# Experts' down rows laid seven to a partition, with every seventh gate and up column as a stationary block

## The reference, cut to what matters

```python
def swiglu(x, w_gate, w_up, w_down):
    return (jax.nn.silu(x @ w_gate) * (x @ w_up)) @ w_down

# moe_swiglu: D_EXPERT = 3584, all float32
for e in range(N_EXPERTS):
    y = y + combine[:, e:e + 1] * swiglu(xt, w_gate[e], w_up[e], w_down[e])
```

## Time and profile before

| | |
|---|---|
| median of 3 runs | 2860.66 us (2859.99 to 2863.47) |
| the profiled execution's own time | 2862.23 us |
| its span, first to last instruction | 2860.5 us |
| mean granted clock of TensorE, as a share of 2.4 GHz | 0.964 |
| PE busy, PEld busy, DVE busy, ACT busy | 93%, 77%, 24%, 15% |
| moved by DMA | 571.23 MB, mean 200 GB/s |

### The profile page before, as it was taken

How to read it: one execution, slowest core, us unless ns; L and a number is a source line. 1 busy time by engine, 2 the same in 40 slices (tenths; PEclk the granted TensorE clock), 3 DMA queues, 4 the chain that set the end, 5 groups by cost and what they waited for, 6 DMA issues and landing times. The chain is left out here.

```text
span 2860.5 us, 76137 instructions
## 1 busy us (share of the span) xinstructions
PE 2653.4 (93%) x34649; PEld 2200.0 (77%) x34649; DVE 673.8 (24%) x1724; ACT 430.1 (15%) x1039; POOL 88.0 (3%) x168
## 2 busy tenths in 40 slices
PE   8899999989989999999999999899989789878998
PEld 7677777768779999989989978666667577766664
DVE  5411000271120110110110111400043576752001
ACT  1111000110110110100110111400012344431000
POOL 0100000010000000000000000000000000010000
PEclk9899999989989999999999999999999798889999
DMA  7334443534339999999999993374541000002442
GB/s 223 113 130 133 132 153 126 166 118 135 145 116 404 407 408 407 407 407 407 407 408 407 407 366 103 98 221 155 173 131 56 5 7 7 4 4 96 148 160 88
DMA packets 290526, 571.23 MB, mean 200 GB/s; under 512 B 18326, under 2 KB 181141, under 8 KB 290405
## 3 DMA queue, kind: packets, MB, share of 16 engines
q1 hardware_dynamic: 290404, 569.49, 55.0%
HBM read 568.37 MB, written 5.28 MB: 201 GB/s over the span
## 5 line engine op out<-in xcount | busy, mean ns | idle before, releaser
L1738 PE MATMUL ps<-xg,ring 128*64 128x80 f32 x14336 | 517.3, 234 | 8.3 <-issue 3.0
L1738 PEld LDWEIGHTS ps<-xg,ring 128*64 128x64 f32 x14336 | 504.3, 137 | 19.4 <-DMA ring<-in_moe_w_up_dram 9.3
L1333 PE MATMUL ps<-xT,ring 128*128 128x256 f32 x1728 | 379.8, 379 | 4.7 <-PEq L452 3.1
L1333 PEld LDWEIGHTS ps<-xT,ring 128*128 128x128 f32 x1728 | 328.0, 190 | 65.9 <-issue 22.4
L1345 PE MATMUL ps<-ring,hidden 128*128 128x512 f32 x688 | 301.8, 592 | 0.0
L1754 PE MATMUL ps<-hidden,expert_down 128*64 128x80 f32 x7168 | 260.0, 233 | 9.7 <-DVE hidden L1830 5.7
L1754 PEld LDWEIGHTS ps<-hidden,expert_down 128*64 128x64 f32 x7168 | 251.9, 137 | 15.7 <-DVE hidden L1830 7.6
L1345 PEld LDWEIGHTS ps<-ring,hidden 128*128 128x128 f32 x688 | 130.7, 190 | 147.5 <-issue 145.4
L618 PE MATMUL ps<-ring,xT 128*128 128x256 f32 (+1 forms) x1056 | 228.2, 379 | 7.5 <-PEq L1214 3.9
L618 PEld LDWEIGHTS ps<-ring,xT 128*128 128x128 f32 x1056 | 198.3, 195 | 36.1 <-issue 9.3
L618 PE MATMUL ps<-xT,ring 128*128 128x256 f32 (+1 forms) x944 | 214.4, 389 | 10.2 <-PEq L596 4.5
(11 more groups left out here) (380 smaller groups left out, 2482.6 us busy)
## 6 DMA issues: line engine op xcount, KB each, us to landing
ring<-in_moe_w_gate_dram SPq DMA_DIRECT2D x128, 896.0 KB, 16.4
ring<-in_moe_w_up_dram SPq DMA_DIRECT2D x128, 896.0 KB, 16.7
expert_down<-in_moe_w_down_dram SPq DMA_DIRECT2D x96, 1024.0 KB, 17.0
ring<-in_mlp_w_dram SPq DMA_DIRECT2D x64, 1024.0 KB, 5.4
ring<-in_w_xkv_dram SPq DMA_DIRECT2D x16, 1024.0 KB, 5.3
expert_down<-in_moe_w_down_dram SPq DMA_DIRECT2D x32, 512.0 KB, 16.5
ring<-in_ffn_w_gate_dram SPq DMA_DIRECT2D x11, 1024.0 KB, 5.3
ring<-in_ffn_w_up_dram SPq DMA_DIRECT2D x11, 1024.0 KB, 5.3
```

The lines of the kernel that those rows point to most:

```text
L1333: mm = pe.matmul(bank[:, m * SEQ:(m + 1) * SEQ], w[:, c, m * P:(m + 1) * P], self.xT[:, c, :], start=(c == 0), stop=(c == KC - 1))
L1738: mm = pe.matmul(bank[b][o:o + HEAD, at, :], w[:, c, f * P + o:f * P + o + HEAD], xg[:, p * E_STEP + c, :], start=(p == 0 and c == 0 and a ...
```

## The change

On the DRAM side, down rows are taken as (chunk k, partition p, block f): row 896k + 7p + f goes to partition p. A partition's rows of a piece are then neighbours in DRAM. To keep the sum right, hidden column 7m + f must stand on partition m of block f, so the stationary operand of block f in gate and up is made of columns f, 7 + f, 14 + f, ..., that is every seventh column of the piece as it lies on chip, 28 bytes apart. The gate and up transfers stay as they are, and so do the number and the sizes of the matmuls, and their order.

```diff
-        self.expert_src = [I[name][0].rearrange("e (c p) f -> e p c f", p=P) for name in ("moe_w_gate", "moe_w_up", "moe_w_down")]
+        self.expert_src = [I[name][0].rearrange("e (c p) f -> e p c f", p=P) for name in ("moe_w_gate", "moe_w_up")]
+
+        self.expert_src.append(I["moe_w_down"][0].rearrange("e (k p f) d -> e p k f d", p=P, f=E_WIDE // P))
...
-    def load_expert_out(self, sp, p, e, rows):
-        src = self.expert_src[2][e, :, rows, :].rearrange("a p c f -> p (a c) f")
+    def load_expert_out(self, sp, p, e, k):
+        first = sum(E_DOWN[:p])
+        src = self.expert_src[2][e, :, k, first:first + E_DOWN[p], :].rearrange("a p b f d -> p (a b f) d")
         sp.dma_start(self.expert_out(p), src).then_inc(self.expert_loaded[2][p].sem, 16)
...
-                        self.load_expert_out(sp, p, e, slice(first, first + E_DOWN[p]) if k is None else bass.ds(k * FB + first, E_DOWN[p]))
+                        self.load_expert_out(sp, p, e, slice(0, 1) if k is None else bass.ds(k, 1))
...
-                                w = self.expert_in(kind, p)
+                                w = self.expert_in(kind, p).rearrange("p c (m f) -> p c f m", f=FB)
...
-                                            mm = pe.matmul(bank[b][o:o + HEAD, at, :], w[:, c, f * P + o:f * P + o + HEAD], xg[:, p * E_STEP + c, :],
+                                            mm = pe.matmul(bank[b][o:o + HEAD, at, :], w[:, c, f, o:o + HEAD], xg[:, p * E_STEP + c, :],
```

More of the change, by code:

```diff
@@ L1478, in expert_ahead_gate @@
         for p in range(len(E_DOWN)):
-            first = sum(E_DOWN[:p])
-            self.load_expert_out(sp, p, slice(0, 1), slice(first, first + E_DOWN[p]))
+            self.load_expert_out(sp, p, slice(0, 1), slice(0, 1))
     def expert_ahead_up(self, sp):
```

## The result

The changed kernel takes 3173.53 us (median of 4 runs, 3172.32 to 3174.76) against 2862.06 us beside it on the same chip (4 runs). The ratio is 1.1089, with a 95% interval from 1.1072 to 1.1107: 11% slower, 311 us more.

A forecast was written before the change was run, and what follows sets the result against it. Weight transfers were taken to bound the expert stage, with TensorE close behind. Stepped loads at 56.0 ns make TensorE the pace, adding 227.6 and 38.4 us, together 266, with the transfers' gain worth nothing: 3127 us, range 2850 to 3390.

The forecast's parts named there:

- The transfers pace the stage, TensorE has 1.5 us of room in a chunk: Expert stage: weight transfers set 27.04 us a chunk; TensorE has only 5.9 us of room an item, 1.5 a chunk.
- the sum: Whole kernel: seven items grow 227.6 us, the first 38.4, together 266 us, giving 3127 us.
- the plateau of 404 to 408 GB/s: Expert stage before the change: the DMA rate was read as 404 to 408 GB/s from slice 13 to 24.
- the item at TensorE's pace: Expert stage before the change: the first item, loaded ahead, was said to run at TensorE's pace, 103.0 us.
- The longer runs are worth 6 us (0 to 8): Down transfers: 24 packets fewer per engine a chunk at 8 ns save 6 us, only while transfers pace the stage.
- A stepped load costs one more column time for each column: Gate and up stationary loads: 0.83 ns more a column, 112 ns a pair, 56.0 ns a load; chance 0.50.
- Two halves keep side by side: Gate and up loads: two halves of 64 columns still overlap when stepped; without overlap a load would take 112 ns.
- The plateau falls to 313 GB/s, transfers land within 7 us, the clock stays: Expert stage, profile after: rate from 407 to 313 GB/s, transfers landing some 7 us or less after issue, clock 1.00.
- The free case: Gate and up loads: stepping is free or hidden and the longer runs pay, 2854 us; chance 0.23.
- The heavier case: Gate and up loads: stepped halves hinder each other, 90 ns more a load, up to 3393 us; chance 0.13.

The follow-up runs named there:

- down_only: Changed kernel with gate and up stationary columns neighbouring again, down rows still seven to a partition: 2853.87 us against 2860.37, ratio 0.9982.
- one_block: Kernel before the change with every seventh column as stationary in only one of seven blocks (64 of 448 loads): 2878.30 us, ratio 1.0065.
- triples: Changed layout with blocks joined in threes instead of a version's twos: pieces (3, 3, 1), runs of 12 KB, step of three words: 2940.04 us, ratio 1.028.
- step_only: Kernel before the change with only the stepped gate and up columns added, down rows as before: 3172.73 us, ratio 1.1096.
- the sweep: Kernel before the change with steps of 1, 2, 3, 4, 5, 7, 8 and 14 words in the eight gate and up pieces: 3064.40 us, one run.
- full_step: Changed kernel with one stationary load of 128 stepped columns instead of two halves of 64 in gate and up: 4047.49 us, one run.
- full_adj: Kernel before the change with one stationary load of 128 neighbouring columns instead of two halves in gate and up: 3255.26 us, one run.

## Why the prediction was right, step by step

- **The transfers pace the stage, TensorE has 1.5 us of room in a chunk.** Borne out: down_only moved with the transfers, one_block filled the room, triples and the change went past it. Two readings on the way were wrong without touching the sum: the plateau of 404 to 408 GB/s ends with slice 23 (slice 24 has 366), and the item at TensorE's pace is the second, with 102.45 us, not the first.
- **The longer runs are worth 6 us (0 to 8).** Measured alone, 6.5 us by the medians (3 to 8 by the ratio) and 4 GB/s. The changed kernel has 12,289 packets fewer, which is 24 x 16 x 32 but for one. And they are worth nothing once TensorE paces the stage: step_only and the change agree within 1 us.
- **A stepped load costs one more column time for each column.** Right in kind, a little small in size: 59.1 ns from load to load where the sum had 56.0. That a column takes one more step was a guess, with a chance of 0.50 and no stepped load in the trace to lean on; the runs bore it out, the working did not prove it. This is the term that was mis-sized. 3.1 ns x 448 loads x 32 chunks = 44 us, and 3127 + 44 = 3171, within 3 us of what was measured. That a stepped column takes about two column times was shown by the sweep and, at the full clock and without two halves, by full_step against full_adj (227 against 112 ns). The surplus is 1.75 instead of 1.67 ns a column, the same in loads of 64 and of 128; where it comes from was not shown, beyond that it differs with the step. The mean duration of a load, 215 ns, was also taken too low (190).
- **Two halves keep side by side.** Yes: 118 ns for both, where 128 stepped columns in one load take 227 at the same clock.
- **The plateau falls to 313 GB/s, transfers land within 7 us, the clock stays.** 300 GB/s, 4.7 to 6.8 us, 1.00.
- **The rivals.** The free case held for the packets alone; for the loads it holds, of the steps that were tried, only at two words. The heavier case, halves that hinder each other by 90 ns a load, did not come: the load grew by 49 ns a pair over the 69 that showed before.

## What to carry to other kernels

An access pattern that makes a transfer's rows longer is paid for where the data is read: here 6 us could be gained on the transfers, and 311 were lost on loads of weights. Count how many of the columns read in turn share 16 bytes. With float32 a step of two words was free, and from four words on a stationary column took about twice its time; so did a moving column at a step of seven words. When a layout asks for a step, look for the smallest one that still gives the long run (two rows a partition, not seven), and work out beforehand how much room the reading engine has.

## What was not expected of the hardware

- A step of 8 bytes costs nothing that shows on stationary loads: 34.3 and 34.6 ns a load at steps of one and two words, 44.1 at three.
- Among steps of four words and more the price still varies, 57.0 ns at five, 61.6 at fourteen.
- The spacing of loads of neighbouring columns followed the granted clock, that of stepped ones didn't. A load of 128 neighbouring columns takes 112 ns from load to load at a granted clock of 1.00 and 210 in a chunk at 0.50. With stepped columns it takes 227 and 231, and the stepped halves took 58.4 ns a load at a mean clock of 0.59 against 59.1 at 1.00. Why they differ was not tested.
- With half the moving columns the mean clock over gate and up fell from 1.00 to 0.59, and the kernel got 27 us slower for doing less.
